# Attention by query tile for both heads, with its output product done in pieces between the attention slots

## The reference

```python
# prompt: 16 heads of 64; a chunk of 64 frames sees itself and the 8 chunks before it
s = einsum('bqhd,bkhd->bhqk', q, k) * 64 ** -0.5 + bias[None]
s = where(valid, s, NEG_INF)
o = einsum('bhqk,bkhd->bqhd', softmax(s), v)
# samples: 16 new frames of each of 8 streams against 256 cached rows and themselves
o = _attend(q, concat(cache_k, k), concat(cache_v, v), bias, None)
h = h + o.reshape(B, T, 1024) @ w_out
```

## Time and profile before

| | |
|---|---|
| median of three runs | 3434.77 us |
| span of the profiled execution | 3431.9 us |
| TensorE busy | 3205.6 us (93%) |
| VectorE, ScalarE, GpSimd busy | 965.8, 809.5, 787.3 us |
| mean granted clock of TensorE | 0.94 of full |
| attention and output product | 1944 to 2538 us of the span |

### The profile page before, as it was taken

How to read it: one execution, slowest core, us unless ns; L and a number is a source line. 1 busy time by engine, 2 the same in 40 slices (tenths; PEclk the granted TensorE clock), 3 DMA queues, 4 the chain that set the end, 5 groups by cost and what they waited for, 6 DMA issues and landing times. The chain is left out here.

```text
span 3431.9 us, 47358 instructions
## 1 busy us (share of the span) xinstructions
PE 3205.6 (93%) x18052; PEld 3025.9 (88%) x18052; DVE 965.8 (28%) x1991; ACT 809.5 (24%) x1491; POOL 787.3 (23%) x566
## 2 busy tenths in 40 slices
PE   6999798779999999998999899999879999999997
PEld 6999576779999999998999676777879999999997
DVE  5111244342121222124111143434342211222214
ACT  3000234222111111113100254545222111111112
POOL 1211023324222322221333000000224222322320
PEclk9999678889999999999999797989989999999998
DMA  8422222211111111110223433333111111111101
GB/s 143 117 89 85 98 84 94 63 31 50 49 37 37 40 58 37 38 29 25 85 85 91 152 115 118 123 114 101 50 31 56 43 37 37 49 49 37 45 22 55
DMA packets 252533, 231.25 MB, mean 67 GB/s; under 512 B 17280, under 2 KB 227792, under 8 KB 252192
## 3 DMA queue, kind: packets, MB, share of 16 engines
q1 hardware_dynamic: 237088, 220.22, 21.7%
q10 hardware_dynamic: 15360, 9.96, 1.0%
HBM read 180.80 MB, written 65.09 MB: 72 GB/s over the span
## 5 line engine op out<-in xcount | busy, mean ns | idle before, releaser
L143 PE MATMUL f_pair_ps<-f_x_hi,f_w_hi 128*128 128x384 f32 x2112 | 707.2, 335 | 12.8 <-POOL f_x_lo L368 12.8
L144 PE MATMUL f_pair_ps<-f_x_hi,f_w_lo 128*128 128x384 f32 x2112 | 706.9, 335 | 0.0
L145 PE MATMUL f_pair_ps<-f_x_lo,f_w_hi 128*128 128x384 f32 x2112 | 706.9, 335 | 0.0
L143 PEld LDWEIGHTS f_pair_ps<-f_x_hi,f_w_hi 128*128 128x128 f32 x2112 | 397.7, 188 | 15.0 <-issue 15.0
L144 PEld LDWEIGHTS f_pair_ps<-f_x_hi,f_w_lo 128*128 128x128 f32 x2112 | 397.6, 188 | 0.0
L145 PEld LDWEIGHTS f_pair_ps<-f_x_lo,f_w_hi 128*128 128x128 f32 x2112 | 397.6, 188 | 0.0
L732 POOL TENSOR_TENSOR f_hid_lo<-f_hid,f_hid_hi 128x384 fp32r<-128x384 f32 x132 | 134.1, 1016 | 1141.2 <-ACT f_hid_hi L707 1141.2
L801 DVE TENSOR_TENSOR res<-res,f_down_ps 128x384 f32<-128x384 f32 x528 | 292.5, 554 | 245.9 <-PE f_down_ps L145 245.9
L794 DVE TENSOR_TENSOR f_hid<-f_gate,f_pair_ps 128x384 f32<-128x384 f32 x132 | 73.2, 554 | 1019.8 <-ACT f_gate L703 1019.8
L145 PE MATMUL f_down_ps<-f_hid_lo,f_w_hi 128*128 128x384 f32 x1056 | 352.7, 334 | 0.0
L143 PE MATMUL f_down_ps<-f_hid_hi,f_w_hi 128*128 128x384 f32 x1056 | 352.7, 334 | 0.0
(11 more groups left out here) (227 smaller groups left out, 4641.8 us busy)
## 6 DMA issues: line engine op xcount, KB each, us to landing
f_stage<-in_ffn_w_gate SPq DMA_DIRECT2D x44, 512.0 KB, 3.8
f_stage<-in_ffn_w_up SPq DMA_DIRECT2D x44, 512.0 KB, 3.8
f_stage<-in_ffn_w_down SPq DMA_DIRECT2D x44, 512.0 KB, 3.5
gla_rows<-in_sums SPq DMA_DIRECT2D x24, 576.0 KB, 3.2
qkv_rows<-qkv_sums SPq DMA_DIRECT2D x24, 576.0 KB, 3.3
in_stage<-in_gla_w_in SPq DMA_DIRECT2D x25, 512.0 KB, 4.6
qkv_stage<-in_w_kv SPq DMA_DIRECT2D x16, 512.0 KB, 4.7
att_k_cache<-in_cache_k SPq DMA_DIRECT2D x64, 128.0 KB, 2.3
```

Source lines behind the costliest of these rows:

```text
L143: pe.matmul(out, w_hi, x_hi, start=first, stop=False)
L144: pe.matmul(out, w_lo, x_hi, start=False, stop=False)
L145: return pe.matmul(out, w_hi, x_lo, start=False, stop=last)
```

## The change

`take` is done by scalar for even numbers of the turned blocks and by vector for odd ones, and each number has its bank; a turn of up to four blocks waits until the one two numbers earlier has been copied. The scores of the two heads are written alternately:

```diff
+                        for c in range(0, w, 512):
+                            n = min(512, w - c)
+                            for head in range(2):
+                                f = slice(head * DH, (head + 1) * DH)
+                                m = pe.matmul(sps[:, head, c:c + n], q[f, b, u * P:(u + 1) * P],
+                                              k[f, b, first + c:first + c + n])
```

The samples of a slot have 32 stationary columns per stream, and write 32 rows of the bank each. In the weighting the turned probabilities are stationary and the values move, 64 columns for each head:

```diff
-                            m = pe.matmul(dst, vr[:, b, i, :], pt[:, v % 2, c], start=n == 0, stop=n == tiles - 1)
+                                m = pe.matmul(dst[:, f], pt[:, s % 2, c:c + P], vr[:, b, u + 1 - w + n, f],
+                                              start=n == 0, stop=n == w - 1)
```

```diff
+    FILL_FIRST = 2 * SLOTS + 3
+    FILL_COUNT = (0, 0, 0, 0, 1, 2, 2, 3, 2, 2)
```

More of the change, by code:

```diff
@@ L1367, in _ @@
                 finish(LAST)
-def attention_core(nc, S, a):
-    with semaphores(nc) as sem:
[L1378 to L1451, removed]
-        kc_in, vc_in = sem("att_kcache_in"), sem("att_vcache_in")
[L1453 to L1460, removed]
@@ L1481, in attention_core @@
[L1481 to L1486, removed]
-            block = ctx.enter_context(nc.Block())
[L1491 to L1496, removed]
+            vc = sb("v_cache", [P, 2, GB, KT_S, P])
@@ L1498, in _ @@
             @block.sync
             def _(sp):
[L1500 to L1505, removed]
-                    for head in range(2):
[L1507 to L1512, removed]
+                zero = STRIP_C + CLIP
@@ L1534, in pair @@
[L1534 to L1538, removed]
[L1539 to L1544 removed]
+                load_rows(0)
@@ L1713, in _, with turn_keys, turn_probs @@
-                pairs(pe, pair)
+                    m.then_inc(turned, 1)
+                def turn_keys(h, g, n):
+                    pe.wait_ge(kc_in, (2 * h + g + 1) * GB * 16)
+                    dst = turn_bank("keys", h, g, n)
+                    for i in range(4):
+                        m = pe.transpose(dst[:, i * P:(i + 1) * P], kc[:, 2 * n + i // 2, i % 2, :], S.ident[:])
+                    m.then_inc(turned, 1)
+                def turn_probs(s, n):
+                    if n == 0:
+                        pe.wait_ge(exped, adds(s + 1))
+                    dst = turn_bank("probs", s, n)
+                    for i, (head, c) in enumerate(blocks(s)[4 * n:4 * n + 4]):
+                        m = pe.transpose(dst[:, i * P:(i + 1) * P], probs[:, s % 2, head, c:c + P], S.ident[:])
+                    m.then_inc(turned, 1)
@@ L1802, in _ @@
+                round_weights(PAIRS - 1)
                 act.wait_ge(cached, PAIRS * 64)
@@ L1849, in _, with add_bias @@
-                pairs(dve, pair)
+                def add_bias(s, head):
+                    h, u = divmod(s, SLOTS)
+                    w = tiles(s) * P
+                    if is_prompt(s):
+                        in1 = bias[:, h % 2, head, WIDE - w:]
+                    else:
+                        first = P if u == NTP else 0
+                        in1 = bias_s[:, h % 2, first:first + w]
+                    if u == 0 and head == 0:
+                        dve.wait_ge(masked, (h + 1) * 5)
+                    dve.wait_ge(scored, adds(s) + head + 1)
+                    if s >= 2 and head == 0:
+                        dve.wait_ge(turned, turned_by(s - 2))
+                    dve.tensor_tensor_reduce(probs[:, s % 2, head, :w], sps[:, head, :w], in1, 1.0, 3e38, ALU.add, ALU.min,
+                                             top[:, s % 3, head:head + 1]).then_inc(biased, 1)
```

741 lines of the change are left out of this document (467 added, 274 removed).

## The result

The changed kernel takes 3459.64 us, the median of 12 runs (3449.06 to 3463.34). The kernel before, timed in turn with it, takes 3441.92 us, also of 12 (3429.39 to 3454.1). The ratio is 1.0049, with a 95% interval of 1.0033 to 1.0065: slower by 0.5%, some 17 us. The forecast was slower by 63 us. One execution of one kernel of the experiments, the one without the product, took 4620.62 us at a mean clock of 0.61 and is left out of that kernel's ratio.

The account below looks back on a forecast made before the run. TensorE bounds attention's wide stretches, latency and a low clock its narrow ones. The stretch goes from 594 to 622 us at full clock, plus 35 for low clock: 657, +63 on 3434.8 gives 3498 us, range 3400 to 3580.

Parts of the forecast that it names:

- the waits: Attention slots: PE waits at output transposes (some 0.6 us) and bank copies behind exponentials; slots 5 to 7 take 8.8, 9.7, 9.9.
- The stores in slot 7: Slot 7 of each pair: scalar issues four stores, which hold it some 2.6 us; the slot takes 9.9 us.
- The weighting with 64 moving columns: Weighting in a wide slot: weight loads set the pace, half the moving columns save nothing, ten blocks take 2.25 us.
- the 31 groups and the last outputs: Behind attention's last slot: the remaining output product groups and the rest of the last outputs take 39 us.
- Rival 2: Slots 5 to 7: waits don't arise because copies overtake in time, and the clock stays up; 3414 us, chance 0.20.
- both heads at once give 2 x 1.08 + 0.20: Scores of a wide tile: the two heads' instructions add up without overlap, plus the change of form, 2.36 us.
- Rival 1: Scores and samples' products: neighbouring heads overlap in part, saving 6.8 us a pair, 54 in all; 3444 us, chance 0.22.
- I take the nearest row, before's own loss, 35: Clock over the replaced stretch: the low clock costs 35 us, as in the kernel before; bounds were none to 160.
- 622 at full clock: The replaced stretch, attention and its output product: the sum of all pairs and the rest, against 594 us before, +28.
- a cold start: Start of attention, pairs 0 and 1: 5 us booked on top of 2 x 70.7 us.
- Rival 3: Wide slots: clock at half through most of them, mean under 0.75 over the stretch; 3623 us, from 3560 on, chance 0.13.
- the pieces as cost: Output product inside attention's slots: a pair with pieces takes 74.7 us, 12.5 of it product, one without 70.7.

Follow-up runs that it names:

- the heads apart: Changed kernel with the two heads' prompt scores one after the other, a one-column full-height product between them; 3618.3 us, ratio 1.0535.
- the three edits: Changed kernel with vector's bias before its first copy, scalar's second copy before its first exponential, output transpose behind the scores, pieces unmoved; 3322.86 us, ratio 0.966.
- the two kernels with all orders changed: Changed kernel with bias first, copy first and transpose behind the scores: 3321.61 us with the output product's pieces spread, 3322.86 us with them gathered.

## Why the prediction was right in its sign and wrong in its size

The measured 3459.6 us lies in the range of 3400 to 3580 and just under the forecast's own, 3460 to 3560. The small difference is not a small effect. It is what two wrong terms leave that nearly cancel, so that the time lies in the range is luck.

**Right: the waits.** The output's transpose waits 0.61 us for scalar (forecast 0.6). Vector's copy, bias and scalar's exponential stand ahead of the bank copy in the order that was worked out, and PE's waits in slots 5 and 6 are 1.51 and 1.54. The stores in slot 7 hold scalar (1.52 at the next transpose). Pieces in a row with one bank wait 0.65 (0.83 forecast). In pair 5, the one nearest to full clock, slots 5 to 7 take 8.6, 10.6 and 8.9 us against 8.8, 9.7 and 9.9 forecast. That comparison has to be made without the two terms that were wrong: less 1.08 for the scores the forecast is 7.7, 8.6 and 8.8, and less 0.45 for each microsecond at 1.2 GHz (clocks of 0.88, 0.78 and 1.00) the measured slots are 7.7, 8.5 and 8.9. So the waits were right to 0.1 us. The weighting with 64 moving columns takes 2.15 for 20 instructions (2.25): half the moving columns saved next to nothing. From the transpose of slot 80 on, the 31 groups and the last outputs take 40.7 us (39 in the sum), and among PE's waits there is none for a transfer, as booked. Rival 2, waits that do not arise, is out.

**Wrong: "both heads at once give 2 x 1.08 + 0.20".** They give 1.28. In the prediction's terms, that saves per pair

- 4 x 1.08 = 4.3 us at the wide tiles,
- 2.15 us at the narrow ones (0.43, 0.63, 0.85 and 1.06 measured for one to four blocks),
- 2.3 us at the samples' scores: eight instructions from 2231.95 to 2232.51 against 1.73 in the earlier trace rows,
- 2.5 us at their weighting: 16 instructions in 0.57, where before's 16 took some 1.8 (1.87 with the tail of the last). These have a quarter of the stationary columns too, and no run takes the two causes apart.

```profile
2231.95 0.64 PE L1704 MATMUL att_score_ps<-att_k_turned,att_q_sample 128*32 128x256 f32 x8
2232.51 0.49 PE L1705 MATMUL att_score_ps<-att_k,att_q_sample 128*128 128x128 f32 x2
...
2240.60 0.64 PE L1740 MATMUL att_out_ps<-att_v_cache,att_p_turned 128*32 128x128 f32 x16
2241.17 0.44 PE L143 MATMUL att_fill_ps<-att_o_hi,att_w_hi 128*128 128x384 f32 x1
```

That is 11.3 a pair, 90 in all. The prompt's share, 52, was tested by the heads apart; the samples' 38 are read from these starts alone. Rival 1 had the mechanism but 54 us. It took the overlap for a quarter of the scores, at the seam of two heads, though the heads' instructions alternate there, so that each has its other half beside it. The Trainium skill ("TensorEngine Tiling (Array Packing)", Key Properties) says that different tiles can load and multiply in parallel; the trace agrees, with 1.06 us for two heads and 1.05 for one. The prediction had weighed this rule and put it at 0.22. No row of before spoke for or against it, so it deserved an even chance and its full size.

**Wrong: "I take the nearest row, before's own loss, 35".** The rows of after give, by 2 (1 - c), 51, 49, 30, 21, 21, 7, 21 and 14 us at 1.2 GHz, 213 in sum, and at 0.45 that is 96 us instead of 35. The 35 left out pair 0 of before, 57.0 us at 0.81; with it before's own loss is 47, and 96 is twice that. The step that failed was to carry a loss over as an amount. Its cause, little streaming and waits, was worked out in the same paragraph and had grown.

**The sum again.** 622 at full clock - 90 + 96 = 628, against 625.1 measured. With the 594 and the scatter of the two executions that is the result. The agreement to 3 us says little, since a price of 0.38 to 0.52 makes 81 to 111 us of the 96, and the 622 holds 5 us for a cold start that the 96 counts again. Rival 3 had the sign of the second error. Its sign in the trace, a mean clock under 0.75 over the stretch, was not met (0.83); it holds in pairs 0 and 1 alone (0.70 and 0.68), those without a piece.

**Wrong: the pieces as cost.** The forecast let a pair with pieces cost 4.0 us more than one without. Measured, pair 3 is 2.1 us shorter than pair 1, and the kernel without any product is only 17 us faster. A dense piece pays for itself in clock where the clock would be low.

What is left open: part of the price of the heads apart, what the samples' narrow products owe to overlap and what to shorter loads, and why equal pairs go at either clock (61.7 and 70.5 us in one execution, 49.9 and 58.6 in two kernels with the same program there).

## What to carry to other kernels

Where one engine works through a queue in order, list for each copy out of a shared bank what stands ahead of it in program order; here three reorderings that change no work took 3.9% off the changed kernel, and that is where a kernel like this is to be mended first. Price such a wait with what it does to TensorE's clock, since here, by an estimate, half of each gain or more came from there, and expect gains of several edits not to add up. When two products use different rows or columns of the array, make them neighbours on purpose and book the overlap in full; when a forecast sits on a property that no row shows, give both outcomes their whole size, for here it was 90 us.

## What the runs showed of the hardware that was not expected

- Products on the two halves of the rows that stand next to each other overlap completely, for fp32 too, where a product is two instructions: 1.06 us for both against 1.05 for one (512 columns), 1.28 for both at 640. On the quarters of the columns eight instructions of 256 columns took 0.56 us against 1.73 over the full width, and 16 of 128 columns 0.57 where 16 of 32 columns over the full width had taken some 1.8. There the stationary operands are narrower as well.
- A busy PE is no warrant of 2.4 GHz. With the heads apart it was busy for 656 of 732 us (90%) at a mean clock of 0.71; with the three edits for 398 of 444 (90%) at 0.99. Unread full-size products put into the waits of after made it 2.4 GHz throughout pairs 3 to 6 and the kernel 59 us faster. A microsecond at 1.2 GHz costs 0.45 us by one pair of before and two of after, 0.42 against the pair with the unread products, 0.52 between two equal pairs with the transpose behind the scores, and 0.38 between the equal pairs 0 of the two kernels with all orders changed. In after no wait of the wide slots of pair 3 is longer than 1.54 us, and the clock fell there even so.
- One column over the full height between two half-height products costs 0.31 us with the changes of form.
